# Split products for every weight chunk of layers 3 and 4: fills between attention steps go from fp32 to three fp32r products

## The chip, the cores and the metric

One core of one Trainium2 chip runs one launch of the whole program. The metric is the device time of that launch in microseconds (us), a median over runs. The engines are named as in the profile: PE is TensorE, DVE is VectorE, ACT is ScalarE, POOL is GpSimd, and SP issues most of the DMAs.

## What is computed

Four layers act on 256 tokens of width 2048, all in float32: a recurrent mixer, a mixture of experts, and then the two layers that the change touches. Cut to these two:

```
def even_layer(x, mem, ...):                     # layer 3
    h = rms_norm_2(x, norm_g) @ w_in
    gq, gk, gv, gb, ga, gg, dq, dk, dv, dg, mq, mg = split_cols(h, EV_SPLITS)
    y = jnp.concatenate([
        gdn_branch(gq, gk, gv, gb, ga, gg, ...),
        diff_attention(dq, dk, dv, dg, ...),     # 8 heads, two softmaxes each, mixed
        memory_attention(mq, mg, mem, ...),      # 4 heads
    ], axis=-1)
    return x + y @ w_out

def odd_layer(x, mem, positions, ...):           # layer 4
    h = rms_norm_2(x, norm_g) @ w_in
    sq, sk, sv, sg, mlq, ckv, kr, mlg, mq, mg = split_cols(h, OD_SPLITS)
    y = jnp.concatenate([
        window_attention(sq, sk, sv, sg, ...),   # 8 heads
        mla_attention(mlq, ckv, kr, mlg, ...),   # 8 heads, width 192
        memory_attention(mq, mg, mem, ...),      # 4 heads
    ], axis=-1)
    return x + y @ w_out
```

## The kernel before, in words

Each engine runs a program of its own, in the order in which it was written; semaphores (the kernel calls them events) tie them together, and the engines meet at the end of every `nc.Block`. All big weights are one stream of units. A unit is 1 MB: four chunks of 128 rows by 512 columns. SP loads units in order into a ring of eight slots (`stream`), and waits with a load until the slot's last unit is used.

A weight chunk is multiplied in one of two ways.

- **In a stage of its own** (`gemm_tokens`). ACT rounds the chunk to fp32r (the high part), DVE subtracts that from the chunk (the low part), and PE adds three fp32r products (high by high, low by high, high by low) for each of two token tiles. That is one step: six matmuls of 512 columns. The features are split in the same way at the start of each such stage. Four chunks of split weights are kept (`SPLIT_DEEP`), and sums of one 512-column block leave PSUM while the next block is multiplied.
- **As a fill** (`Fill`). A list of blocks of 512 columns is worked off in small portions that other stages call: `fill.multiply(pe, steps)` puts the next steps into PE's program, `fill.store_act` and `fill.store_dve` put the stores of finished blocks into the others'. A fill step multiplies the chunk straight from the ring in fp32, two matmuls of 512 columns, and asks nothing of ACT and DVE. There is one pair of PSUM banks for it, so PE waits at the start of a block until the last block has been stored.

`head_norm` normalizes heads (DVE squares, sums, scales), `times_silu` applies a gate and turns the result into features (`Turned`), and `attention` handles two heads at a time. One turn of it reads, per engine:

- PE: scores of two heads; fill portion 0; transposes of the next two heads' queries and keys (`begin`); portion 1; transposes of the probabilities; portion 2; sums with the values; portion 3. `steps=(a, b, c, d)` gives the sizes of the portions.
- DVE: scale, bias and maximum of two heads; store 0; stage the next two heads' queries and keys; store 1; for differential attention, mix the two softmaxes; store 2; write the outputs; store 3.
- ACT: exponentials; store 0; copy the transposed queries and keys; store 1; copy the transposed probabilities; stores 2 and 3.

The order of layer 3 is: the GDN branch, `gemm_tokens` over six blocks for the differential branch (96 steps), `head_norm`, `attention` (four turns), `head_norm` with gate, then memory attention (`head_norm`, two turns, `times_silu`) and a last `gemm_tokens` of 16 steps. In layer 4: `gemm_tokens` of 80 steps, window attention (`head_norm`, two calls of two turns, `times_silu`), `gemm_tokens` of 64 steps, a small product for the rotary key (`SmallProduct`, L2329), `gemm_tokens` of 16 steps, `head_norm`, `mla_rope`, `attention` (four turns), `times_silu`, `gemm_tokens` of 32 steps for the memory keys, memory attention, and `gemm_tokens` of 48 steps.

## Time and profile before

| what | value |
|---|---|
| time, median of 3 runs | 2788.83 us (2786.02 to 2790.07) |
| profiled execution, first to last instruction | 2787.4 us |
| PE busy with matmuls | 2598.2 us (93% of the span) |
| DVE busy | 1354.9 us (49%) |
| ACT busy | 976.6 us (35%) |
| HBM traffic | 189 GB/s over the span |

The profile gives no separate time for the profiled execution beyond its span; the median of the runs is 1.4 us above that span. Busy time counts the time that at least one instruction of an engine is in flight, and the ends of matmuls are modelled, so where PE's pace matters, the distance between starts is read and not the length of one. The first stage that the change touches begins at 1703 us of the span. An fp32 matmul of 512 columns stands in the trace as two records, an fp32r matmul as one. Idle time in the trace names who ended it; an engine name with a q is that engine's sequencer (a semaphore without an instruction, or the meeting at the end of a block).

### The profile page before, as it was taken

How to read it: one execution, taken by the hardware profiler on the slowest of the kernel's cores; microseconds unless marked ns; L12 is line 12 of the kernel's file. 1: busy time of each engine (PE TensorE's matmuls, PEld its weight loads, DVE VectorE, ACT ScalarE, POOL GpSimd, SP SyncE). 2: the span in 40 equal slices, each digit the busy share in tenths (PEclk: the TensorE clock that was granted, in tenths of full speed). 3: DMA queues.
4: the chain of work that ended last, by engine and by line, in shares of the span. 5: the costliest groups of instructions: out<-in, count | busy, mean ns of one | idle time of the engine just before them, and what ended most of it. 6: DMA issues, size and time to landing. Idle time of an engine off the chain costs nothing. (4 is left out here: it accounts for less than half of the span.)

```text
span 2787.4 us, 38289 instructions
## 1 busy us (share of the span) xinstructions
PE 2598.2 (93%) x14362; PEld 1770.8 (64%) x14362; DVE 1354.9 (49%) x2599; ACT 976.6 (35%) x1730; POOL 105.2 (4%) x117
## 2 busy tenths in 40 slices
PE   8999999999888889999998999989899989988999
PEld 7984555887544444448975766855467746845757
DVE  5654784665311112226764545554535445464535
ACT  5544122444122122225524424432235414423424
POOL 0001111020011100010000000000000000001000
PEclk9999999999999999999999999999999989999999
DMA  7754433554499999984431114543334523431432
GB/s 302 216 211 156 138 138 141 186 199 147 160 422 422 422 421 422 399 344 161 169 122 67 38 57 166 189 173 106 106 136 141 200 85 141 154 122 75 148 109 91
DMA packets 80312, 529.66 MB, mean 190 GB/s; under 512 B 9089, under 2 KB 13569, under 8 KB 18849
## 3 DMA queue, kind: packets, MB, share of 16 engines
q1 hardware_dynamic: 76128, 514.50, 48.9%
q0 software_dynamic: 3456, 11.02, 1.6%
q8 instruction: 99, 1.62, 0.2%
q10 hardware_dynamic: 576, 2.10, 0.2%
q14 instruction: 53, 0.43, 0.1%
HBM read 520.24 MB, written 7.34 MB: 189 GB/s over the span
## 5 line engine op out<-in xcount | busy, mean ns | idle before, releaser
L379 DVE TENSOR_TENSOR split_wl<-ring,split_wh 128x512 fp32r<-128x512 f32 x480 | 331.0, 698 | 227.5 <-ACT split_wh L353 225.7
L353 ACT ACTIVATE split_wh<-ring 128x512 fp32r<-128x512 f32 x480 | 301.0, 631 | 291.6 <-PE ps L329 291.6
L327 PE MATMUL ps<-split_wh,split_xh 128*128 128x512 f32 x960 | 375.5, 391 | 0.0
L329 PE MATMUL ps<-split_wh,split_xl 128*128 128x512 f32 x960 | 373.6, 389 | 0.0
L328 PE MATMUL ps<-split_wl,split_xh 128*128 128x512 f32 x960 | 373.5, 389 | 0.0
L2132 PE MATMUL ps<-ring,yT 128*64 128x256 f32 x2048 | 247.8, 387 | 52.4 <-DMA ring<-in_weights 48.3
L631 PE MATMUL ps<-ring,xT 128*128 128x512 f32 x512 | 241.8, 625 | 29.9 <-issue 7.2
L434 PE MATMUL ps<-features_xh,features_wh 128*128 128x256 f32 x832 | 236.7, 285 | 1.5 <-DVE features_wl L425 1.5
L2132 PEld LDWEIGHTS ps<-ring,yT 128*64 128x64 f32 x2048 | 137.7, 137 | 155.4 <-DMA ring<-in_weights 91.0
L436 PE MATMUL ps<-features_xh,features_wl 128*128 128x256 f32 x832 | 235.3, 283 | 0.0
L631 PE MATMUL ps<-ring,yT 128*128 128x512 f32 x448 | 206.3, 612 | 20.9 <-issue 11.1
L999 PE MATMUL ps<-ring,xT 128*128 128x512 f32 x512 | 222.0, 592 | 2.8 <-PEq L451 1.7
L329 PEld LDWEIGHTS ps<-split_wh,split_xl 128*128 128x128 f32 x960 | 180.2, 188 | 37.5
L327 PEld LDWEIGHTS ps<-split_wh,split_xh 128*128 128x128 f32 x960 | 180.2, 188 | 37.4
L328 PEld LDWEIGHTS ps<-split_wl,split_xh 128*128 128x128 f32 x960 | 180.2, 188 | 37.3
L631 PEld LDWEIGHTS ps<-ring,xT 128*128 128x128 f32 x512 | 99.5, 200 | 150.7 <-issue 142.2
L425 DVE TENSOR_TENSOR features_wl<-ring,features_wh 128x512 fp32r<-128x512 f32 x208 | 139.4, 691 | 83.3 <-ACT features_wh L419 79.5
L419 ACT ACTIVATE features_wh<-ring 128x512 fp32r<-128x512 f32 x208 | 130.2, 630 | 133.5 <-PE ps L436 133.5
L999 PEld LDWEIGHTS ps<-ring,xT 128*128 128x128 f32 x512 | 97.1, 190 | 120.6 <-issue 118.1
L631 PEld LDWEIGHTS ps<-ring,yT 128*128 128x128 f32 x448 | 84.6, 195 | 123.4 <-issue 123.3
L434 PEld LDWEIGHTS ps<-features_xh,features_wh 128*128 128x128 f32 x832 | 159.6, 192 | 2.9 <-DVE features_wl L425 2.6
L436 PEld LDWEIGHTS ps<-features_xh,features_wl 128*128 128x128 f32 x832 | 159.6, 192 | 0.0
(630 smaller groups left out, 3389.9 us busy)
## 6 DMA issues: line engine op xcount, KB each, us to landing
ring<-in_weights SPq DMA_DIRECT2D x468, 1024.0 KB, 5.1
x_res<-in_x SPq DMA_DIRECT2D x1, 2048.0 KB, 7.5
yT<-in_mem SPq DMA_DIRECT2D x1, 2048.0 KB, 15.7
rel_skew<-lru_feat POOLq DMA_DIRECT2D x1, 2048.0 KB, 50.7
mem_features<-yT ACTq DMA_DIRECT2D x4, 512.0 KB, 6.6
s_wb<-in_s_bc POOLq DMA_DIRECT2D x4, 512.0 KB, 4.0
s_wc<-in_s_bc POOLq DMA_DIRECT2D x4, 512.0 KB, 3.9
gate_bias<-in_gate_bias POOLq DMA_DIRECT2D x8, 256.0 KB, 3.9
```

What stands on the lines that cost most here:

```text
L327: nc.tensor.matmul(out, xh[:, kc, at], wh[:, c % deep, :], start=kc == 0, stop=False)
L328: nc.tensor.matmul(out, xh[:, kc, at], wl[:, c % deep, :], start=False, stop=False)
L329: last = nc.tensor.matmul(out, xl[:, kc, at], wh[:, c % deep, :], start=False, stop=kc == chunks - 1)
L353: nc.scalar.activation(wh[:, c % deep, :], raw(unit, turn, c), ACT.Copy).then_inc(w_high.sem, 1)
L379: last = nc.vector.tensor_tensor(wl[:, c % deep, :], raw(unit, turn, c), wh[:, c % deep, :], ALU.subtract)
L419: self.k.nc.scalar.activation(self.wh[:, c % self.deep, :], self.k.ring[:, slot, c * BLK:(c + 1) * BLK], ACT.Copy)\
L425: self.k.nc.vector.tensor_tensor(self.wl[:, c % self.deep, :], self.k.ring[:, slot, c * BLK:(c + 1) * BLK], self.wh[:, c % self.deep, :], ...
L434: nc.tensor.matmul(out, self.wh[:, c, cols], self.xh[:, kc, :], start=kc == 0, stop=False)
L436: last = nc.tensor.matmul(out, self.wl[:, c, cols], self.xh[:, kc, :], start=False, stop=kc == KC - 1)
L631: last = nc.tensor.matmul(k.ps[:, 6 + t, :], x[:, kc, t * P:(t + 1) * P], k.ring[:, slot, c * BLK:(c + 1) * BLK], start=kc == 0, stop=kc = ...
L999: mm = nc.tensor.matmul(k.ps[:, 6 + t, :], k.xT[:, kc, t * P:(t + 1) * P], k.ring[:, slot, c * BLK:(c + 1) * BLK], start=kc == 0, stop=kc ...
L2132: last = nc.tensor.matmul(k.ps[s * WIN:(s + 1) * WIN, p, 0:FF], window[:, p, kc, :], k.ring[:, slot, at:at + FF], start=kc == 0, stop=kc = ...
```

## The change

The features of a layer are split into high and low parts once (`k.layer`) and stay split. Every `gemm_tokens` that reads them takes them as they are (`whole=`). All fills except those of the GDN branch become `SplitFill`: a fill step is now three fp32r products per token tile, as in `gemm_tokens`, with the high part of each weight chunk made by ACT and the low part by DVE. These are put into the two engines' programs at the places where they stored blocks before. The buffer of split chunks is four deep, and at each such place the engines work up to four steps (`LEAD`) beyond what PE's portion has reached. Some blocks move from `gemm_tokens` stages into fills: two of the six blocks of the differential branch (its gate), two of the four blocks of MLA's input, and the product of MLA's output with `w_out`. The rotary key's small product moves to the end of the first `gemm_tokens` of layer 4. From layer 3 on the ring has four slots; the split features lie where the other four were.

Fill steps, before and now:

| place | before | now |
|---|---|---|
| layer 3, `head_norm` of differential attention | 8 | 8 |
| its four turns, portions (4,3,3,2), now (5,4,4,3) | 48 | 64 |
| its second `head_norm` | 8 | 8 |
| memory attention: norm, two turns, silu | 6 + 20 + 6 | 8 + 32 + 8 |
| layer 4, window: norm and bias, four turns, silu | 10 + 20 + 2 | 16 + 44 + 4 |
| MLA: norm and rope, four turns, silu | 20 + 8 + 4 | 22 + 36 + 6 |
| memory attention: norm, two turns, silu | 6 + 20 + 6 | 6 + 20 + 6 |
| all fills | 192 | 288 |
| all `gemm_tokens` steps from 1703 us on | 352 | 256 |

The core of the diff:

```
-def gemm_tokens(k, x, blocks, upb, finish_act, finish_dve, dve_after_act=False, ahead=None, deep=SPLIT_DEEP, beside=None, after=None):
+def gemm_tokens(k, x, blocks, upb, finish_act, finish_dve, dve_after_act=False, ahead=None, deep=SPLIT_DEEP, beside=None, after=None,
+                into=None, whole=None, parts=None, product=None):
...
+        if whole is not None:
+            xh, xl = whole
...
+class SplitFill:
+    LEAD = SPLIT_DEEP
...
+    def multiply(self, pe, steps):
...
+            if kc == 0:
+                pe.wait_ge(fill_a.sem, fill_a.at(n - 1))
+                pe.wait_ge(fill_v.sem, fill_v.at(n - 1))
...
+            pe.wait_ge(w_low.sem, w_low.at(step))
+            for t in range(NT):
+                out, at = k.ps[:, 6 + t, :], slice(t * P, (t + 1) * P)
+                mm(out, xh[:, kc, at], wh[:, c, :], start=kc == 0, stop=False)
+                mid = mm(out, xh[:, kc, at], wl[:, c, :], start=False, stop=False)
+                last = mm(out, xl[:, kc, at], wh[:, c, :], start=False, stop=kc == chunks - 1)
...
+            last.then_inc(w_used.sem, 1)
...
+    def make_highs(self, act, upto):
...
+        for step in range(self.high_at, min(upto, self.total)):
+            while self.act_done < len(self.blocks) and self.first[self.act_done + 1] <= step - self.LEAD:
+                self.take_act(act)
+            act.wait_ge(w_used.sem, w_used.at(step - SPLIT_DEEP))
...
+            k.nc.scalar.activation(k.parts[0][:, c, :], k.ring[:, slot, c * BLK:(c + 1) * BLK], ACT.Copy).then_inc(w_high.sem, 1)
...
+    def make_lows(self, dve, upto):
...
+            dve.wait_ge(w_high.sem, w_high.at(step))
+            k.nc.vector.tensor_tensor(k.parts[1][:, c, :], k.ring[:, slot, c * BLK:(c + 1) * BLK], k.parts[0][:, c, :], ALU.subtract)\
+                .then_inc(w_low.sem, 1)
...
+    def store_dve(self, dve, steps):
+        self.dve_at += steps
+        self.make_lows(dve, self.dve_at + self.LEAD)
...
-    gemm_tokens(k, k.xT, 6, KC // UNIT_KC, *store_tokens(k, pd))
+    gemm_tokens(k, None, 4, KC // UNIT_KC, *store_tokens(k, pd), whole=k.layer, parts=k.parts)
...
-              fill=fill, steps=(4, 3, 3, 2), turned=free.rearrange("p (j a) -> p j a", j=2))
+              fill=fill, steps=(5, 4, 4, 3), turned=free.rearrange("p (j a) -> p j a", j=2))
...
-        gemm_tokens(k, k.xT, 4, KC // UNIT_KC, *store_tokens(k, pq), ahead=lambda sp: load(k, sp, kr_w, k.dram["mla_kr_w"]))
+        gemm_tokens(k, None, 2, KC // UNIT_KC, *store_tokens(k, pq, 2 * BLK), whole=k.layer, parts=k.parts)
...
-    gemm_tokens(k, k.yT[:, 8:20, :], D // BLK, 3, *add_to_x(k, k.xT), dve_after_act=True,
+    gemm_tokens(k, None, D // BLK, 1, *add_to_x(k, out_spare), dve_after_act=True, whole=k.layer, parts=k.parts,
```

The first place shown is one turn of differential attention. First DVE's queue, from the second head's scores to the mix; `pe_b` is the event of the scores, `act_b` that of the exponentials. Before:

```order
L2740 SCALAR_TENSOR_TENSOR att_scores<-ps,diff_bias 128x512 [waits pe_b]
L2740 SCALAR_TENSOR_TENSOR att_scores<-ps,diff_bias 128x512
L2749 TENSOR_REDUCE att_stat<-att_scores 128x4
L2754 TENSOR_SCALAR att_stat<-att_stat 128x4
L2803 TENSOR_TENSOR att_q<-diff_q,rows_sb 128x256
L2803 TENSOR_TENSOR att_k<-diff_in,rows_sb 128x256
L2803 TENSOR_TENSOR att_q<-diff_q,rows_sb 128x256
L2803 TENSOR_TENSOR att_k<-diff_in,rows_sb 128x256
L2769 RECIPROCAL att_stat<-att_stat 128x4 [waits act_b]
```

The same place of DVE's queue now (`parts_wl` are low parts of weight chunks, `w_high` is the event of their high parts):

```order
L2937 SCALAR_TENSOR_TENSOR att_scores<-ps,diff_bias 128x512 [waits pe_b]
L2937 SCALAR_TENSOR_TENSOR att_scores<-ps,diff_bias 128x512
L2946 TENSOR_REDUCE att_stat<-att_scores 128x4
L2951 TENSOR_SCALAR att_stat<-att_stat 128x4
L804 TENSOR_TENSOR parts_wl<-ring,parts_wh 128x512 [waits w_high] x5
L3000 TENSOR_TENSOR att_q<-diff_q,rows_sb 128x256
L3000 TENSOR_TENSOR att_k<-diff_in,rows_sb 128x256
L3000 TENSOR_TENSOR att_q<-diff_q,rows_sb 128x256
L3000 TENSOR_TENSOR att_k<-diff_in,rows_sb 128x256
L804 TENSOR_TENSOR parts_wl<-ring,parts_wh 128x512 [waits w_high] x3
L3155 COPY diff_in<-ps 128x512 [waits fill_a,w_used]
L804 TENSOR_TENSOR parts_wl<-ring,parts_wh 128x512 [waits w_high]
```

The staging of the next heads now stands behind five low parts, and the mix (the next row, L2966) behind four more and the store of a block.

Next ACT's queue in a turn of the same attention, before (`dve_b` is DVE's event that the scores are scaled, `pe_a` and `pe_c` are PE's transposes):

```order
L2702 ACTIVATE att_scores,att_stat<-att_scores,att_stat 128x256 [waits dve_b]
L2702 ACTIVATE att_scores,att_stat<-att_scores,att_stat 128x256 x3
L2702 ACTIVATE att_scores,att_stat<-att_scores,att_stat 128x256 [waits dve_b]
L2702 ACTIVATE att_scores,att_stat<-att_scores,att_stat 128x256 x3
L2692 ACTIVATE yT<-ps 128x512 [waits pe_a] x2
L2712 ACTIVATE yT<-ps 128x512 [waits pe_c] x2
```

And now (`parts_wh` are high parts; `w_used` is PE's event that a step is done):

```order
L2899 ACTIVATE att_scores,att_stat<-att_scores,att_stat 128x256 [waits dve_b]
L2899 ACTIVATE att_scores,att_stat<-att_scores,att_stat 128x256 x3
L783 ACTIVATE parts_wh<-ring 128x512 [waits unit_loaded3,w_used] x4
L783 ACTIVATE parts_wh<-ring 128x512 [waits unit_loaded0,w_used]
L2889 ACTIVATE yT<-ps 128x512 [waits pe_a] x2
L783 ACTIVATE parts_wh<-ring 128x512 [waits unit_loaded0,w_used] x3
L3152 ACTIVATE diff_in<-ps 128x512 [waits w_used]
L783 ACTIVATE parts_wh<-ring 128x512 [waits unit_loaded1,w_used]
L2909 ACTIVATE yT<-ps 128x512 [waits pe_c] x2
```

High parts now stand between the exponentials and every later operation of the turn, each with a wait for a step of PE four steps earlier.

## Rows read from the trace of the kernel before

**Rows 1.** Windows: two `gemm_tokens` stages; busy us (count) of PE, PEld, DVE, ACT, POOL.

```profile
1703.50:1834.20 130.70, 130.70 (x578) 108.27 (x577) 72.33 (x104) 64.24 (x103) 0.00 (x0) 1.00 0.54 193
2716.50:2782.00 65.50, 65.50 (x290) 54.24 (x289) 38.39 (x56) 32.20 (x52) 0.00 (x0) 1.00 0.24 89
```

**Rows 2.** Page, costliest groups: low and high parts of weight chunks.

```profile
L379 DVE TENSOR_TENSOR split_wl<-ring,split_wh 128x512 fp32r<-128x512 f32 x480 | 331.0, 698 | 227.5 <-ACT split_wh L353 225.7
L353 ACT ACTIVATE split_wh<-ring 128x512 fp32r<-128x512 f32 x480 | 301.0, 631 | 291.6 <-PE ps L329 291.6
```

**Rows 3.** Timeline, end of a `gemm_tokens` step: start, length, engine, operation.

```profile
1820.41 0.39 PE L329 MATMUL ps<-split_wh,split_xl 128*128 128x512 f32 x1
1820.64 0.39 PE L327 MATMUL ps<-split_wh,split_xh 128*128 128x512 f32 x1
1820.84 0.63 ACT L353 ACTIVATE split_wh<-ring 128x512 fp32r<-128x512 f32 x1 [0.67 <-PE ps L329]
1821.50 0.69 DVE L379 TENSOR_TENSOR split_wl<-ring,split_wh 128x512 fp32r<-128x512 f32 x1 [0.61 <-ACT split_wh L353]
```

**Rows 4.** Windows, the stages with fills, layer 3, then layer 4.

```profile
1839.20:1857.30 18.10, 15.69 (x33) 6.61 (x33) 15.80 (x16) 1.38 (x2) 0.00 (x0) 0.90 0.65 225
1857.30:1972.60 115.30, 107.43 (x384) 56.52 (x384) 49.63 (x110) 30.00 (x86) 0.00 (x0) 0.99 0.31 109
1972.60:2004.60 32.00, 30.08 (x82) 14.71 (x82) 24.40 (x34) 8.08 (x10) 0.00 (x0) 0.95 0.35 126
2004.60:2070.20 65.60, 61.30 (x202) 32.67 (x202) 18.45 (x42) 15.63 (x33) 0.00 (x0) 0.97 0.29 102
2226.40:2249.00 22.60, 20.59 (x40) 8.50 (x40) 13.76 (x10) 0.22 (x1) 0.00 (x0) 0.87 0.51 177
2249.00:2334.50 85.50, 71.64 (x274) 42.71 (x274) 35.06 (x102) 25.56 (x64) 0.00 (x0) 0.92 0.21 74
2462.00:2508.20 46.20, 36.83 (x80) 15.63 (x80) 28.99 (x51) 3.93 (x7) 0.00 (x0) 0.93 0.26 91
2508.20:2589.50 81.30, 68.38 (x298) 40.47 (x299) 36.14 (x93) 28.02 (x63) 9.59 (x16) 0.96 0.19 71
2637.00:2648.10 11.10, 10.54 (x24) 4.48 (x24) 8.47 (x15) 1.50 (x2) 0.00 (x0) 1.00 0.26 79
2648.10:2714.50 66.40, 61.41 (x203) 33.08 (x203) 19.09 (x43) 15.68 (x34) 0.00 (x0) 0.97 0.30 103
```

**Rows 5.** Timeline, one turn of differential attention (from scores to scores).

```profile
1887.81 2.00 PE L2650 MATMUL ps<-yT 64*128 64x256 f32 x16
1888.99 1.29 DVE L2740 SCALAR_TENSOR_TENSOR att_scores<-ps,diff_bias 128x512 f32<-128x512 f32 x2 [4.09 <-PE ps L2650]
1889.73 7.13 PE L631 MATMUL ps<-ring,xT 128*128 128x512 f32 x16
...
1894.83 0.51 ACT L2702 ACTIVATE att_scores<-att_scores,att_stat 128x256 f32<-128x256 f32 x1 [0.87 <-DVEq L2758]
1894.88 0.42 DVE L2803 TENSOR_TENSOR att_q<-diff_q,rows_sb 128x256 f32<-128x256 f32 x1
1896.64 0.18 DVE L2769 RECIPROCAL att_stat<-att_stat 128x4 f32<-128x4 f32 x1
1896.70 0.38 PE L2637 MATMUL ps<-ident_sb,att_q 128*128 128x128 f32 x2
...
1898.74 0.18 DVE L2769 RECIPROCAL att_stat<-att_stat 128x4 f32<-128x4 f32 x1
...
1914.07 2.00 PE L2650 MATMUL ps<-yT 64*128 64x256 f32 x16
```

**Rows 6.** Timeline, memory attention: PE's wait for a block's store, and the matmuls behind it.

```profile
2652.13 3.60 PE L631 MATMUL ps<-ring,yT 128*128 128x512 f32 x8
...
2658.33 2.98 PE L631 MATMUL ps<-ring,yT 128*128 128x512 f32 x4 [2.61 <-issue]
```

**Rows 7.** Windows of 4 us around that wait.

```profile
2654.00:2658.00 4.00, 1.73 (x5) 0.42 (x3) 1.91 (x4) 2.01 (x7) 0.00 (x0) 1.00 0.27 61
2658.00:2662.00 4.00, 3.67 (x9) 1.95 (x10) 2.00 (x7) 0.00 (x0) 0.00 (x0) 0.64 0.48 201
```

More of the change, by code:

```diff
@@ L200, in load @@
         else:
[L201 removed]
+            src = k.dram["weights"][ds(turn * slots + unit, 1)].rearrange("u p n -> p (u n)")
         sp.dma_start(k.ring[:, slot], src).then_inc(k.unit_loaded[slot], 16)
[L204 to L211 removed]
+    while first < upto:
+        slots, _ = ring_of(first)
+        end = min(upto, LATE) if first < LATE else upto
+        turns = (end - first) // slots if first < LATE or first >= LATE + LATE_RING else 0
+        if turns >= 2:
+            with sp.Fori(0, turns) as i:
+                for s in range(slots):
+                    load(first + s, i)
+            first += turns * slots
+        else:
+            load(first)
+            first += 1
@@ L1689, in moe_places, with times_mem_gain @@
     return features[:, :, :], keys[:, :, :]
-def times_mem_gain(k, pool, features, gain):
+def times_mem_gain(k, pool, features, gain, chunks=range(KC)):
     pool.wait_ge(k.loaded, k.loads)
-    for c in range(KC):
+    for c in chunks:
         part = slice(c, c + 1)
@@ L2470, in _ @@
                 dve.drain()
+                if fill:
+                    fill.lows(dve, steps)
                 at = 0
@@ L2493, in _ @@
             def _(act):
+                if fill:
+                    fill.highs(act, min(steps, 6 + 2 * len(parts)))
                 act.wait_ge(ms.sem, ms.at(0))
@@ L2621, in _ @@
             def _(pool):
-                if beside is not None:
-                    beside(pool)
+                for i in range(turns):
+                    if beside is not None:
+                        beside(pool, i)
             @block.tensor
@@ L2922, in memory_keys, with memory_attention @@
     kv = k.sb(scope, f"{tag}_kv", [P, NT, 2 * MEM_HEADS * P])
-    gemm_tokens(k, features, 2, KC // UNIT_KC, *store_tokens(k, kv))
+    gemm_tokens(k, features, 2, KC // UNIT_KC, *store_tokens(k, kv), parts=k.parts)
     return kv
-def memory_attention(k, tag, qg, kv, gain_q, gain_k, fill):
+MEM_STEPS = {"evm": (8, (5, 5, 4, 2), 8), "odm": (6, (3, 3, 2, 2), 6)}
+def memory_attention(k, tag, qg, kv, gain_q, gain_k, fill, out):
     n = MEM_HEADS * P
+    first, steps, last = MEM_STEPS[tag]
     with ExitStack() as inner:
```

312 lines of the change are left out of this document (222 added, 90 removed).

## Prediction, made before the run

> **What bounds the kernel now.** I read the profile's page first (PE busy 93% of the span), then PE's timeline from 1703 us on to find the stages, then one row of windows per stage, and last one attention turn on all three engines. The reader is to see four things.
>
> PE never stops in a `gemm_tokens` stage: 130.7 us for 96 steps and 65.5 us for 48 [rows 1]. So a split step costs PE 1.36 us there, while ACT and DVE, at 0.63 and 0.70 us for it [rows 2], have slack.
>
> An fp32 fill step is four records, 0.43 us apart (16 records, 7.13 us with the modelled tail [rows 5]): 1.72 us of PE and nothing of ACT or DVE.
>
> In an attention turn PE is nearly always at work, because DVE's and ACT's chains run under its portions. The turn shown lasts 26.3 us (1887.81 to 1914.07): 12 steps of 1.72 and 5.4 of attention matmuls make 26.0. DVE's statistics for two heads take 5.9 us (1888.99 to 1894.88), under portion 0; staging ends at 1896.64, before PE asks at 1896.70; the mix follows at once, 2.1 us a head, under portion 1 [rows 5].
>
> In the stages of `head_norm` DVE is as long as PE: 15.8 busy of 18.1 us in the first [rows 4].
>
> **The change on PE alone.** All 544 steps stay. 192 fill steps fall from 1.72 to 1.36: -69 us. 96 steps change place at the same price. If PE stayed the bound, that would be all: 2720.
>
> **What it does to the order.** A step's split chunk goes into the place of the step four before it. At each store place ACT and DVE make parts up to four steps beyond PE's portion, and the last of these needs PE's last step of that portion. Both engines are in order, so whatever stands behind a store place starts only when PE has finished the portion. The refill chain is in [rows 3]: PE's step ends at 1820.64, ACT starts at 1820.84, DVE at 1821.50 and is done at 1822.19: 1.55 us. Thus what ran under PE's portions now runs after them, and PE, whose four ready chunks are spent, waits for it.
>
> The Trainium skill ("TensorE: Matmul & The Clock Gate", the table at its top) says that ScalarE's and VectorE's queues are strictly first in, first out. Going by that rule no later staging or mix can pass a waiting low part, which speaks against this change; if they could pass, the time would be the 2720 above. The turn's rows agree as far as they go: every operation starts in program order [rows 5].
>
> **One turn of differential attention, portions 5, 4, 4, 3.** T is the start of the scores.
> - DVE is free of its last low part at T+1.6, has both heads' statistics at +7.5 (5.9), ACT the exponentials at +9.5 (four, 2.1). Only then comes the fifth chunk's high part: ready with its low part at +10.9. PE, after 1.9 of scores and four steps, stood there at +7.3: wait 3.6. Portion 0 ends at 12.3.
> - Refill 1.55, staging 0.9 a head (1.76 for two [rows 5]): transposes from 14.8 to 16.1, 2.9 of it waiting.
> - Portion 1, 5.4, with one block end in it. High part, copy, low part, copy: 2.3 us (ACT 0.6 and 0.6, DVE 0.7 and 0.7, 0.2 before). To 23.8.
> - Refill 1.55, mix 2.1 a head, the second transposes behind it: to 30.0, 5.3 waiting.
> - Portion 2, values, portion 3: 5.4 + 1.8 + 4.1, to 41.3.
>
> Three turns of 41.3, the last without staging 37.6, 2 for splitting the GDN features between them, 5 for head and tail: 168.5 where 115.3 stood [rows 4]: **+53**.
>
> **The other attentions.** Their softmax is divided after the sums, so PE waits for no mix. Left are the staging wait (3; 4.4 in window attention, where four high parts stand behind the exponentials) and the block ends: 2.9 where a block is added to x; before it cost 2.6 [rows 6]. A turn is 5.4 of attention (9.9 in MLA) plus steps times 1.36 plus these.
> - Layer 3 memory: turns 33.4 and 31.7, silu 14.5, ends 4.4: 84.0 against 65.6: **+18.4**, for 14 more steps.
> - Window: 2 x (25.3 + 21.6), one inner block end 2.3, silu 11.2, ends 6.5: 113.8 against 85.5: **+28.3**, 26 more.
> - MLA: 3 x 25.5 + 20.1, block ends 6.1, ends and POOL's gain beside it 9.6, silu 14.9: 127.2 and 0.5 for the meeting, against 81.3: **+46.4**, 30 more.
> - Layer 4 memory, no more steps: 24.8 + 21.6 + 19.6 = 66.0 against 66.4: **-0.4** [rows 4].
>
> **The norms.** DVE's low parts, 0.62 us each back to back (0.70 with the latency [rows 2]), add to a DVE that already sets the end. First norm: 12 of them (8 and 4 ahead) 7.5, first chunk's chain 1.3, last refill partly: **+9.5**. The two norms of the row at 1972.6: 2 x 8 low parts 9.9, less 0.7 in which DVE waited: **+9.2**. Window norm and bias: 20 low parts 12.4, less 6 of idle on DVE (13.8 of 22.6 busy), and a copy: **+6.7**. MLA norm and rope: 12 low parts in the norm, +8.2; in rope PE's steps stand behind 6.7 us of DVE sums but the store that came after rope comes earlier, +2.7: **+10.9**. Layer 4 memory: 10 low parts and the first chain: **+7.0** [rows 4].
>
> **Moved out of the bound stages.** 96 `gemm_tokens` steps, as many as the first row: **-130.7** [rows 1]. The features' splits at stage starts hide behind warm-up matmuls: 0. The rotary product no longer overlaps a norm's sums but stands behind a stage, about +6 there and -3 where it was: **+3.2**.
>
> **Sum:** 53 + 18.4 + 28.3 + 46.4 - 0.4 + 9.5 + 9.2 + 6.7 + 10.9 + 7.0 + 3.2 - 130.7 = **+61.5 us**.
>
> **The clock.** Behind a PE wait of 2.61 us four records take 2.98 us; eight took 3.60 before it. The granted clock of that stretch is 0.64, part of it at 1.2 instead of 2.4 GHz, after 1.00 [rows 6, 7]. At half pace a stretch of some 4 us does 2 us of work, so it costs about 2. New waits as long as that: some 12 in differential attention, some 10 elsewhere. Bounds: none of them lowers the clock further (0), or each costs 2 (+44). Rows 4 have granted clocks of 0.87 to 1.00 with such waits in them already, and cold stretches inside a later wait cost nothing, so I take +12.
>
> The Trainium skill (same title, "What's actually happening") says that the throttled state is the default and that only activity releases it. If that rule bites at every such wait, the time is 2787.4 + 61.5 + 44 + 1.4 = 2894; the one wait shown agrees [rows 7].
>
> **Result:** 2787.4 + 61.5 + 12 = 2861 for the profiled span; the runs' median is 1.4 above the span: **2862 us**.
>
> **Rivals.**
> - *PE stays the bound* (faster, 2720 to 2785). It needs that parts are ready ahead of PE's portions. The stalls in my sum are 61.5 + 69 = 130 us; the change breaks even when they are under 69, about half. For it speaks that low parts cost half a step on DVE and attention's DVE work leaves 65 us of 115 free [rows 4]; against it, that the free time lies under PE's portions, where the order now lets nothing but refills run. Chance 0.11, and 0.03 for within 0.2%.
> - *The waits are real but lighter* (2795 to 2835): block ends and refills overlap more, the clock costs nothing. +61.5 less a third of the norms' and block ends' 50 is +45; with fewer staging waits +20. Chance 0.16.
> - *The clock pays for every wait* (2885 to 2920): +61.5 and up to 44, or more where slow portions delay refills. 0.10.
> - *A ring of four starves* (over 2890): a unit of 1 MB is used up in four steps, 5.4 us, and 193 GB/s were moved at that pace with eight slots [rows 1]. One us of wait per unit over the 72 units of the fills: +72 more. For it: half the lead. Against: four units are still 22 us of PE. 0.03.
> - *The order does not change* is excluded: the queues show it.
>
> My forecast, 2835 to 2885, has the rest, 0.57. The range 2812 to 2898 takes in the zero clock term and most of its upper bound and leaves out the faster side and the far end. A difference under 0.2% (5.6 us) is what a measurement of this kernel can't tell from none. Faster 0.11, same 0.03, slower 0.86.
>
> **What would show it.** PE idle before the fifth matmul step of portion 0, before the staged transposes and before the transposed probabilities in differential attention, ended by DVE, 12 us and more a turn; turns of 40 us or more. Other attentions with one staging wait a turn. Norm stages ended by DVE. Three `gemm_tokens` stages shorter by 43.6 us each at unchanged pace. More windows of low granted clock. Wrong would be: portions that run on while DVE stages, or low parts that come well before PE needs them.

## The result, and the profile after

| kernel | time, median | ratio to before, 95% interval | profiled span | mean granted clock |
|---|---|---|---|---|
| before | 2789.1 us (2786.0 to 2790.1) | | 2787.4 us | 0.985 |
| after | 2907.8 us (2905.3 to 2909.4) | 1.0428 [1.0414, 1.0443] | 2903.6 us | 0.961 |

The change makes the kernel 119 us slower. The forecast was 2862 us, 73 us slower, with a range up to 2898: the direction was right, the time lies 10 us beyond the range.

The page of the changed kernel: span, busy times, the clock in 40 slices of the span, and the three groups of the fills' split steps.

```profile
span 2903.6 us, 39591 instructions
...
PE 2589.0 (89%) x14740; PEld 1879.6 (65%) x14740; DVE 1471.9 (51%) x2795; ACT 1087.1 (37%) x1922; POOL 107.4 (4%) x117
...
PEclk9999999999999999999999999788999999988989
...
L759 PE MATMUL ps<-parts_wh,layer_xh 128*128 128x512 f32 x576 | 253.9, 441 | 96.6 <-DVE parts_wl L804 43.0
L804 DVE TENSOR_TENSOR parts_wl<-ring,parts_wh 128x512 fp32r<-128x512 f32 x288 | 192.8, 694 | 249.1 <-ACT parts_wh L783 247.7
...
L783 ACT ACTIVATE parts_wh<-ring 128x512 fp32r<-128x512 f32 x288 | 175.1, 628 | 270.3 <-PE ps L761 253.5
```

No engine is the bound: PE waits for a low part (L804), DVE for a high part (L783), ACT for PE's step (L761). A part costs ACT and DVE the same 0.63 and 0.69 us as in [rows 2]; what changed is who waits for whom. The clock row has a 7 and two 8s where layer 3's differential attention stands.

The stages with fills, as windows: the same stages in the same order as [rows 4] (columns as there), without the `gemm_tokens` stretches between them. Here a stage reaches to the first matmul of the next, so some lengths hold up to 6 us more than the same stage in [rows 4]; the attention named below has the same edges in both.

```profile
1786.80:1817.80 31.00, 14.20 (x55) 11.03 (x53) 24.82 (x33) 10.43 (x17) 0.00 (x0) 0.83 0.51 174
1817.80:2007.20 189.40, 138.74 (x576) 106.91 (x576) 92.62 (x176) 71.01 (x153) 0.00 (x0) 0.83 0.24 87
2007.20:2052.10 44.90, 30.00 (x123) 24.10 (x123) 36.77 (x54) 19.11 (x29) 0.00 (x0) 0.86 0.28 103
2052.10:2144.90 92.80, 80.37 (x349) 64.84 (x349) 45.29 (x83) 40.31 (x75) 0.00 (x0) 0.90 0.31 114
2297.00:2342.00 45.00, 32.69 (x161) 26.95 (x159) 28.64 (x35) 13.52 (x23) 0.00 (x0) 0.89 0.42 143
2342.00:2466.60 124.60, 104.98 (x485) 84.89 (x485) 64.34 (x148) 54.07 (x113) 0.00 (x0) 0.92 0.28 104
2545.20:2605.90 60.70, 38.79 (x139) 28.84 (x137) 48.30 (x85) 21.31 (x36) 0.00 (x0) 0.86 0.26 91
2605.90:2742.90 137.00, 113.30 (x513) 86.88 (x513) 67.95 (x140) 56.84 (x113) 11.68 (x16) 0.91 0.27 99
2787.80:2806.90 19.10, 9.95 (x44) 7.65 (x42) 15.92 (x27) 7.64 (x13) 0.00 (x0) 0.92 0.16 62
2806.90:2876.30 69.40, 58.31 (x264) 46.84 (x265) 34.36 (x67) 30.96 (x60) 0.00 (x0) 0.90 0.30 106
```

Differential attention takes 189.4 us instead of 115.3 [rows 4], and PE is busy 138.7 of them. Its work there is 64 steps of 1.36 and four times 5.4, that is 108.6. So 50.7 us are idle, and 30 us are PE at work but slow. The granted clock of the row is 0.83; it was 0.99.

One turn of it, on three engines (start, length, engine, operation, idle time before it and who ended it):

```profile
1867.44 2.00 PE L2847 MATMUL ps<-yT 64*128 64x256 f32 x16
...
1874.76 0.39 PE L761 MATMUL ps<-parts_wh,layer_xl 128*128 128x512 f32 x1
1878.30 0.50 PE L759 MATMUL ps<-parts_wh,layer_xh 128*128 128x512 f32 x1 [3.15 <-DVE parts_wl L804]
...
1879.17 0.63 PE L759 MATMUL ps<-parts_wh,layer_xh 128*128 128x512 f32 x1
1879.60 0.63 PE L760 MATMUL ps<-parts_wl,layer_xh 128*128 128x512 f32 x1
1880.03 0.63 PE L761 MATMUL ps<-parts_wh,layer_xl 128*128 128x512 f32 x1
...
1880.70 0.63 ACT L783 ACTIVATE parts_wh<-ring 128x512 fp32r<-128x512 f32 x1 [1.62 <-PE ps L761]
1881.36 0.69 DVE L804 TENSOR_TENSOR parts_wl<-ring,parts_wh 128x512 fp32r<-128x512 f32 x1 [1.31 <-ACT parts_wh L783]
1881.97 0.42 DVE L3000 TENSOR_TENSOR att_q<-diff_q,rows_sb 128x256 f32<-128x256 f32 x1
1882.80 0.69 PE L2834 MATMUL ps<-ident_sb,att_q 128*128 128x128 f32 x2 [2.14 <-DVEq L2928]
...
1891.55 0.47 PE L759 MATMUL ps<-parts_wh,layer_xh 128*128 128x512 f32 x1 [2.09 <-ACT diff_in L3152]
...
1896.88 1.12 PE L2865 MATMUL ps<-ident_sb,att_scores 128*128 128x128 f32 x4 [3.36 <-DVEq L2977]
...
1898.95 1.11 PE L2865 MATMUL ps<-ident_sb,att_scores 128*128 128x128 f32 x4 [0.96 <-DVEq L2977]
...
1912.71 2.00 PE L2847 MATMUL ps<-yT 64*128 64x256 f32 x16
```

The reader is to see the chain that the prediction drew: PE's last step of the portion, then ACT's high part, DVE's low part, only then DVE's staging (L3000), and PE's transposes (L2834) behind it. The four waits stand where they were forecast, and are 3.15, 2.14, 2.09 and 3.36 + 0.96 = 11.7 us in this turn, where the prediction had 3.6, 2.9, 2.3 and 5.3 = 14.1. But the turn takes 45.3 us and not 41.3 (its neighbours 47.7 and 46.9), because behind the waits records stand 0.43 us apart and not 0.23 (1879.17, 1879.60, 1880.03): 1.2 GHz and not 2.4.

The same over everything from the first changed stage to the last, before and after:

```profile
1703.50:2782.00 1078.50, 1005.87 (x3964) 688.23 (x3963) 546.65 (x955) 395.68 (x730) 9.59 (x16) 0.97 0.38 134
```

```profile
1699.50:2898.30 1198.80, 997.95 (x4343) 796.96 (x4342) 663.82 (x1151) 505.53 (x922) 11.68 (x16) 0.91 0.35 124
```

Idle time rose from 72.6 to 200.8 us: +128.2 (the prediction's stalls were 130). PE's work should have fallen by 69 and fell by 7.9: +61 of slow matmuls. -69 + 128 + 61 = +120; the first changed stage began 4 us earlier, which makes the +116 of the two spans. So at a first look the clock, for which the prediction had put 12 us and at most 44, is half of the loss. A busy time does not say, though, whether a slow matmul delays anything: that is for the experiments.

### The profile page after: what moved, and what is told of

The parts are those of the page before. It is cut to its first block and busy times, and to the rows that moved or that the text cites. A ratio compares the mean times of both kernels' runs of the same rounds, so it can differ in the third digit from the quotient of the medians.

```text
span 2903.6 us, 39591 instructions
## 1 busy us (share of the span) xinstructions
PE 2589.0 (89%) x14740; PEld 1879.6 (65%) x14740; DVE 1471.9 (51%) x2795; ACT 1087.1 (37%) x1922; POOL 107.4 (4%) x117
## 5 line engine op out<-in xcount | busy, mean ns | idle before, releaser
L759 PE MATMUL ps<-parts_wh,layer_xh 128*128 128x512 f32 x576 | 253.9, 441 | 96.6 <-DVE parts_wl L804 43.0
L804 DVE TENSOR_TENSOR parts_wl<-ring,parts_wh 128x512 fp32r<-128x512 f32 x288 | 192.8, 694 | 249.1 <-ACT parts_wh L783 247.7
L783 ACT ACTIVATE parts_wh<-ring 128x512 fp32r<-128x512 f32 x288 | 175.1, 628 | 270.3 <-PE ps L761 253.5
L760 PE MATMUL ps<-parts_wl,layer_xh 128*128 128x512 f32 x576 | 243.0, 422 | 0.0
L761 PE MATMUL ps<-parts_wh,layer_xl 128*128 128x512 f32 x576 | 241.4, 419 | 0.0
L1178 PE MATMUL ps<-ring,xT 128*128 128x512 f32 x512 | 222.0, 592 | 2.8 <-PEq L488 1.7
L759 PEld LDWEIGHTS ps<-parts_wh,layer_xh 128*128 128x128 f32 x576 | 119.3, 207 | 139.0 <-DVE parts_wl L804 50.7
L413 DVE TENSOR_TENSOR split_wl<-ring,split_wh 128x512 fp32r<-128x512 f32 x208 | 145.1, 707 | 97.6 <-ACT split_wh L387 96.6
L387 ACT ACTIVATE split_wh<-ring 128x512 fp32r<-128x512 f32 x208 | 130.9, 633 | 131.7 <-PE ps L360 131.7
L413 DVE TENSOR_TENSOR parts_wl<-ring,parts_wh 128x512 fp32r<-128x512 f32 x176 | 120.0, 691 | 94.4 <-ACT parts_wh L387 94.1
L387 ACT ACTIVATE parts_wh<-ring 128x512 fp32r<-128x512 f32 x176 | 109.7, 632 | 113.5 <-PE ps L360 106.8
L761 PEld LDWEIGHTS ps<-parts_wh,layer_xl 128*128 128x128 f32 x576 | 119.2, 207 | 27.8
L472 PE MATMUL ps<-features_xl,features_wh 128*128 128x256 f32 x448 | 126.7, 283 | 0.0
```

The costliest lines, as they stand in the source:

```text
L387: nc.scalar.activation(wh[:, c % deep, :], raw(unit, turn, c), ACT.Copy).then_inc(w_high.sem, 1)
L413: last = nc.vector.tensor_tensor(wl[:, c % deep, :], raw(unit, turn, c), wh[:, c % deep, :], ALU.subtract)
L759: mm(out, xh[:, kc, at], wh[:, c, :], start=kc == 0, stop=False)
L760: mid = mm(out, xh[:, kc, at], wl[:, c, :], start=False, stop=False)
L761: last = mm(out, xl[:, kc, at], wh[:, c, :], start=False, stop=kc == chunks - 1)
L783: k.nc.scalar.activation(k.parts[0][:, c, :], k.ring[:, slot, c * BLK:(c + 1) * BLK], ACT.Copy).then_inc(w_high.sem, 1)
```

## The experiments

All times are medians; where not said otherwise the computation is unchanged. In the edits, comments behind a `#` are this document's. "Loss" is what the change adds to the kernel before.

**Filler matmuls in the waits.** Two runs, differing in the number of fillers:

```diff
+                    if fill and n == 0 and comps == 2:
+                        fill.multiply(pe, SPLIT_DEEP)
+                        keep_busy(k, pe, 0, 12)        # second run: 8
+                        fill.multiply(pe, steps[0] - SPLIT_DEEP)
...
+                        keep_busy(k, pe, 0, 8)         # second run: 5
                         begin(i + 1)
...
+                    def at_block_end():
+                        if more:
+                            pe.wait_ge(qk_copied.sem, qk_copied.at(0, i + 1, 2))
+                        keep_busy(k, pe, 0, 8)         # second run: 4
...
+                            pe.wait_ge(shifted.sem, shifted.at(j, i, 2))
+                            keep_busy(k, pe, 2 + 2 * j, (13, 4)[j])   # second run: (7, 3)
                             pe.wait_ge(mixed.sem, mixed.at(j, i, 2))
```

> The changed kernel with nothing taken away: PE gets more instructions. In the attentions it runs filler matmuls (128x256, 0.23 us each warm) in places where it waits: 12 ahead of the fifth step of a differential turn, 8 ahead of the staged transposes, 8 at a block end in portion 1, 13 and 4 ahead of the two heads' transposed probabilities. Theory (half of the loss is idle time, half is the clock that falls behind each wait): the waits stay, but the matmul records behind them are 0.23 us and not 0.43; the differential attention falls from 189 to about 165 us, the kernel by about 35 us (20 to 50), to about 2873. Rival (the slow steps lie under DVE's chains and cost nothing, all of the loss is waits): within 6 us of the changed kernel, 2908. A filler that outlasts its wait would make it slower.

2897.2 us, 1.0381 [1.0363, 1.0398]: 11 us less than the changed kernel, nearer to the rival's number, and it proves nothing either way, since I had put a filler at 0.23 us where it takes 0.43 (it is two records). In the turn from 1871.49 us PE was never idle and the records of the steps stood 0.23 us apart, but the fillers took 20 us a turn for 12 us of waits. The turn stayed at 47.0.

> The first filler run again with shorter fillers: there each filler matmul took 0.43 us and not the 0.23 that I had put, so the fillers (5.3, 3.6, 3.6, 5.8 and 1.9 us in a turn) outlasted the waits of 3.1, 2.1, 2.1, 3.4 and 1.4 us while every record of PE ran at 0.23. Now 8, 5, 4, 7 and 3 of them: 3.5, 2.2, 1.7, 3.0 and 1.3 us. Theory (about half of the loss is the clock behind the waits): a differential turn falls from 46.9 to about 42 us, the differential attention by 18 to 24 us, the kernel by about 30, to 2878 (2862 to 2890). Rival (cold steps lie under the other engines' chains): 2897 or more, as in the first filler run.

2868.3 us, 1.0284 [1.0267, 1.0301]: 39.5 us less than the changed kernel, with more work for PE. Of the timeline of one turn:

```profile
1862.67 2.00 PE L2853 MATMUL ps<-yT 64*128 64x256 f32 x16
...
1870.22 3.61 PE L293 MATMUL ps<-rows_sb,ident_sb 128*128 128x256 f32 x16
...
1875.05 2.32 PE L293 MATMUL ps<-rows_sb,ident_sb 128*128 128x256 f32 x10
...
1886.56 3.18 PE L293 MATMUL ps<-rows_sb,ident_sb 128*128 128x256 f32 x14
...
1904.10 1.14 PE L2853 MATMUL ps<-yT 64*128 64x256 f32 x8
```

From scores to scores it is 41.4 us: with the clock kept up (L293 are the fillers; the granted clock of this attention is 0.99), the turn is the 41.3 that the prediction summed for the order alone. Part of that match is luck. The five gaps that the fillers stand in measure 3.3, 2.3, 2.3, 3.5 and 1.6 us, 13.0 in sum, where the prediction had 14.1 of waits, and the work between them is 28.5 us, where it had 27.2. The gaps are also 1 us longer than the 12.0 us that PE waits in an average turn of the changed kernel: a slow PE comes later to its waits and waits less there, so part of what the slow records cost is given back. The clock in the attentions costs 39.5 us of the 119 by the medians, and 33.6 by the spans of the two profiled runs. Where a filler outlasts its wait, the clock's cost is more than that.

**Parts two steps ahead, not four.** At the first two store places of a differential turn, the first of the others:

```diff
-        self.make_lows(dve, self.dve_at + self.LEAD)
+        self.make_lows(dve, self.dve_at + lead)        # 2 at these places, 4 at the others; ACT the same
```

> The changed kernel, where in an attention turn ACT and DVE split only two steps beyond PE's portion at its first store place (in differential attention at its first two) and not four; the rest of the parts follow behind the staging and the mix. Theory (the last refills, which need PE's last steps, hold up staging and mix): the wait before the staged transposes falls by about 1 us a turn, that before the transposed probabilities by about 2.5, a differential turn by about 4.5 us; 13 to 15 us there, about 1.2 us a turn over 11 turns elsewhere, with a few us of clock: about 25 us (15 to 40) less, 2883. Rival (DVE's own work is the chain and refills wait for nothing): no change, 2908.

2847.7 us, 1.0214 [1.0194, 1.0234]: 60 us less, more than twice what I expected. One turn:

```profile
1867.94 0.79 PE L759 MATMUL ps<-parts_wh,layer_xh 128*128 128x512 f32 x1 [3.14 <-DVE parts_wl L804]
...
1870.67 0.52 PE L2835 MATMUL ps<-ident_sb,att_q 128*128 128x128 f32 x2
...
1879.37 0.66 PE L2866 MATMUL ps<-ident_sb,att_scores 128*128 128x128 f32 x4 [0.23 <-DVEq L2978]
```

The wait ahead of the staged transposes is gone and the one ahead of the transposed probabilities fell from 3.36 to 0.23 us; the turn is 36.3 to 38.7 us. All waits of a turn together fell from 12.0 to 6.2 us on average, and that took almost 9 us off it (37.8 on average, after 46.6). The other 3 us fit the slow stretches that stood behind those waits; no run separates the two.

**The ring of four alone.**

```diff
+LATE_RING = 4
+LATE = sum(b * u for _, b, u in STREAM[:[name for name, _, _ in STREAM].index("ev_mem_v")])
...
+    return (RING, 0) if unit < LATE else (LATE_RING, LATE)
```

> The kernel before, with the weight ring of layers 3 and 4 cut from eight slots to four as in the change, and nothing else. Theory (four units are still over 20 us of PE): no change, 2789 within 4 us. Rival (a ring of four starves PE): PE waits for the ring's loads in the gemm stages and the fills, 20 us or more slower.

2787.1 us, 0.999 [0.9981, 1.0]: no cost in the kernel before, whose late units (from `ev_mem_v` on) now use four slots. In the changed kernel's own trace no wait of PE, ACT or DVE from 1699.5 us on is put down to a load. That rival of the prediction is excluded.

**The moved blocks as fp32 products.** The changed kernel's order; this run leaves the features' low parts out of the fills' products:

```diff
-                mm(out, xh[:, kc, at], wh[:, c, :], start=kc == 0, stop=False)
-                mid = mm(out, xh[:, kc, at], wl[:, c, :], start=False, stop=False)
-                last = mm(out, xl[:, kc, at], wh[:, c, :], start=False, stop=kc == chunks - 1)
+                last = mm(k.ps[:, 6 + t, :], xh[:, kc, t * P:(t + 1) * P].bitcast(F32), k.ring[:, slot, c * BLK:(c + 1) * BLK],
+                          start=kc == 0, stop=kc == chunks - 1)
```

> The changed kernel's order and its moved blocks, but each fill step is one fp32 product of the features' high parts with the ring's weights, as before the change; the weights are not split in the fills, so ACT and DVE make no parts there, and the features' low parts are left out of these products. Theory (the loss comes from the refills in order and the clock behind their waits, not from the move): 96 moved steps at 0.36 us more are +35 on the kernel before, less up to 25 us of PE's idle time in window and latent attention that they fill: about 2810 (2798 to 2826). Rival (the move itself, its block ends and the loads, makes the waits): over 2850.

2819.3 us, 1.0109 [1.0092, 1.0126]. The move alone costs 30 us, almost all of 96 steps at 0.36 us more; the idle time of layer 4 that it might have filled was hardly filled. The split products, which save PE 104 us against this kernel (288 steps at 0.36 less), cost 88 us on top.

**No parts in the fills.** ACT and DVE split only the first four chunks of each fill, and PE multiplies these again and again, so what the fills compute is not the product of the weights; the run serves for its time alone.

```diff
-            act.wait_ge(w_used.sem, w_used.at(step - SPLIT_DEEP))
...
-            k.nc.scalar.activation(k.parts[0][:, c, :], k.ring[:, slot, c * BLK:(c + 1) * BLK], ACT.Copy).then_inc(w_high.sem, 1)
+            if step < SPLIT_DEEP:
...
+                k.nc.scalar.activation(k.parts[0][:, c, :], k.ring[:, slot, c * BLK:(c + 1) * BLK], ACT.Copy).then_inc(w_high.sem, 1)
```

> The changed kernel with the fills' part work left out: ACT and DVE split only the first four weight chunks of each fill, and PE multiplies these over and over, with its full number of fp32r products and its waits for the loads; what it computes in the fills is thus not the product of the weights. Theory (the whole loss is the parts' order and work; PE's own work is 69 us less than before): 2720 to 2745, the time that the first rival of the prediction gives. Rival (something else in the change costs time, such as the moved blocks' ends, the ring or fp32r products beside the attentions): 2780 or more.

2753.2 us, 0.9874 [0.9858, 0.9889]: the making and placing of parts costs 155 us, all of the loss and more. It also corrects the first rival: with parts for nothing the change would gain 36 us, not 69. From the first changed stage to the last:

```profile
1700.30:2745.90 1045.60, 950.32 (x4344) 769.54 (x4343) 487.91 (x879) 343.94 (x651) 10.32 (x16) 0.97 0.40 142
```

PE idles 95.3 us where it idled 72.6, and is busy 950.3 where it was busy 1005.9, 55.6 less and not 69. A likely reason for the idle time, not tested, is that a shorter step covers less of the statistics, mixes and norms beside it.

**Another place for the parts.** A table for each attention says how PE's steps are dealt to the four portions, and up to which step of the turn DVE and ACT have made parts at each of 8 and 7 points (ahead of, between and behind the two heads' statistics, stagings, mixes, and so on). The table came from adding up the three queues with the durations of the rows. Work, depth of the parts and number of steps stay. A finished block is also stored one part earlier than in the changed kernel, in this run and in the next.

```diff
-              fill=fill, steps=(5, 4, 4, 3), turned=free.rearrange("p (j a) -> p j a", j=2))
+              fill=fill, steps=(5, 4, 4, 3), turned=free.rearrange("p (j a) -> p j a", j=2), plan=((7, 7, 2, 0), (0, 6, 7, 7, 12, 15, 19, 20), (6, 9, 10, 17, 11, 16, 9)))
...
                     for j in pair:
+                        dve_parts(dve, i, j)    # make_lows up to the table's step, ahead of head j's statistics
...
-            while self.dve_done < len(self.blocks) and self.first[self.dve_done + 1] <= step - self.LEAD:
+            while self.dve_done < len(self.blocks) and self.first[self.dve_done + 1] <= step - 3:
```

> The changed kernel with the same work, the same four-deep parts and the same PE steps per turn, but another order inside the attentions: PE's steps are dealt to the four portions anew (differential attention 7, 7, 2, 0 for 5, 4, 4, 3), and ACT and DVE make parts at more places of a turn (between the two heads' statistics, exponentials, stagings and mixes), nowhere parts whose slots come free only with PE's last steps ahead of work that PE waits for; a filled block is evicted one part earlier. Theory (the loss is the place of the refills in two strictly ordered queues, and the clock behind the waits, not the parts' work): by adding up the three queues with the rows' durations a differential turn falls from 41 us (47 with the clock) to about 30, the other attentions by 8, 17, 18 and 6 us, so with the clock about 110 us less than the changed kernel: 2800 (2775 to 2835), about the kernel before. Rival (ACT's and DVE's part work is what PE waits for, wherever it stands): no better than two steps of lead gave, 2848 or more.

2782.0 us, 0.9979 [0.9969, 0.9989]: 126 us less than the changed kernel, 0.2% less than before. The first of the plan's three lists deals PE's steps. Differential attention as a window, and PE's wait at a block end in a turn, the only one over 0.5 us left in it:

```profile
1819.40:1953.80 134.40, 122.29 (x586) 99.24 (x587) 94.02 (x178) 69.84 (x154) 0.00 (x0) 0.93 0.35 126
```

```profile
1870.57 0.47 PE L759 MATMUL ps<-parts_wh,layer_xh 128*128 128x512 f32 x1 [1.84 <-ACT diff_in L3175]
```

134 us instead of 189, with DVE and ACT as busy as in the changed kernel (94.0 and 69.8 against 92.6 and 71.0). So in this attention the engines' work was never the bound, the order was.

> The fifth run's kernel, but PE's portions are those of the change (5, 4, 4, 3 in differential attention); only the places at which ACT and DVE make their parts differ from the changed kernel. Theory (it is the refills' place, not the split of PE's steps): the queues' sums give 13 us more than the fifth run in differential attention and about 8 in the others: 2803 (2790 to 2820), so 105 of the 126 us come from the places alone. Rival (the dealing of PE's steps did it): within 15 us of what two steps of lead gave, 2833 or more.

2804.0 us, 1.0064 [1.0048, 1.0079], 1 us from the expectation. With PE's portions left at 5, 4, 4, 3 and as they were in the other attentions, the places of the parts, with the earlier store of a block, give 104 of the 126 us. What the earlier store alone gives was not measured.

**Fillers in the norms.**

```diff
                     fill.multiply(pe, steps)
+                    keep_busy(k, pe, 5, hold)          # 16, 10 or 14; 12 or 4 ahead of the transposes in a gating
...
+                    if i == 0:
+                        keep_busy(k, pe, 0, 5)         # at the start of each attention
```

> The reordered kernel of the fifth run with filler matmuls (0.43 us each) where PE still waits long in and between the norms: 16 at the end of the first norm of layer 3, 12 ahead of the transposes of the second, 10 at the end of each memory norm, 14 at the end of the latent norm, 4 ahead of the transposes in two gatings, 5 at the start of each attention. Theory (each of some 10 long waits is followed by a stretch at half pace): 1 to 2 us each, together 8 to 20 us less than 2782: about 2768 (2760 to 2776), below the kernel before by 0.7%. Rival (the cold steps behind these waits lie under DVE's chains of the first turn, or the fillers outlast their waits): 2780 or more.

2781.4 us, 0.9976 [0.9967, 0.9985]: nothing, the rival's case. The two profiled runs, without and with these fillers:

```profile
core 0: 2784.3 us, clock 0.976
```

```profile
core 0: 2783.4 us, clock 0.985
```

The mean clock is back where it was before the change, and the time has not moved. The rival named two reasons, and the two traces show some of each. The first norm, up to the first scores, is 35.8 us and not 33.6; 1.5 of that is the five fillers at the start of the attention, which outlast their wait. The first differential turn behind it, now free of its slow start, is 32.3 us and not 33.4, so little of that start had cost time. Up to the next `gemm_tokens` stage layer 3 is 3.4 us shorter, and the segment of MLA is 2.6 us longer. How the rest divides was not taken apart. A mean clock is no measure of what the clock costs.

**Low parts by POOL in the norms.** In the norms, the bias stage and the rotary stage POOL makes the low parts, 84 of the 288 by the trace (the expectation says some 50); DVE's own calls there then find none left to make.

```diff
+            @block.gpsimd
+            def _(pool):
+                if isinstance(fill, SplitFill):
+                    fill.pool_lows(pool, steps)        # the same subtraction by gpsimd.tensor_tensor
```

> The reordered kernel of the fifth run, where the low parts of the fills are made by POOL and not by DVE in the norms, the bias stage and the rotary stage (some 50 of 288); all other low parts stay on DVE. In these stages DVE sets the end: they are 8, 13, 9, 12 and 6 us longer than in the kernel before. POOL's nearest row is 1.06 and 0.61 us for a product of 128x256, so one low part may take 1.2 to 2.1 us, against 1.36 of PE. Theory (DVE's part work in the stages that it bounds is the rest of the loss): 25 to 35 us less than 2782: about 2752 (2742 to 2765). Rival (POOL and DVE slow one another when both read two tensors, or POOL's low parts become the chain that PE waits for): DVE's squares and sums take longer by as much as is taken off it, 2775 or more.

2791.1 us, 1.0005 [0.9996, 1.0014]: 9 us slower than the run without it (7 by the two ratios, since the two were measured beside separate runs of the kernel before). The groups of the first norm, POOL's and DVE's of this run, then DVE's of the run without:

```profile
L832 POOL TENSOR_TENSOR parts_wl<-ring,parts_wh 128x512 fp32r<-128x512 f32 x12 | 21.2, 1797 | 560.6 <-ACT parts_wh L783 560.6
...
L2687 DVE TENSOR_TENSOR diff_q<-diff_q,head_stat 128x1024 f32<-128x1024 f32 x2 | 4.5, 2292 | 0.1
...
L2670 DVE TENSOR_TENSOR yT<-diff_in 128x1024 f32<-128x1024 f32 x2 | 4.2, 2104 | 0.1
```

```profile
L2667 DVE TENSOR_TENSOR diff_q<-diff_q,head_stat 128x1024 f32<-128x1024 f32 x2 | 2.4, 1222 | 0.1
L2650 DVE TENSOR_TENSOR yT<-diff_in 128x1024 f32<-128x1024 f32 x2 | 2.4, 1222 | 0.1
```

DVE's products of two tensors take 2.1 to 2.3 us beside POOL's and 1.22 without. That is the first half of the rival, and in layer 3 it does not outweigh the gain: from the first norm to the next `gemm_tokens` stage the run is 3.3 us shorter. The loss is in layer 4, 3.8 us in the window segment and 2.4 in that of MLA. In the window segment the second half of the rival shows:

```profile
2253.10 9.85 POOL L832 TENSOR_TENSOR parts_wl<-ring,parts_wh 128x512 fp32r<-128x512 f32 x6
2254.31 2.58 DVE L2687 TENSOR_TENSOR swa_in<-swa_in,head_stat 128x1280 f32<-128x1280 f32 x1
2263.30 0.77 PE L759 MATMUL ps<-parts_wh,layer_xh 128*128 128x512 f32 x1 [3.55 <-PEq L2656]
```

DVE is done with the norm at 2256.9 and POOL only at 2263.0, and the block ends with POOL. PE, after a wait of 3.55 us there, runs the steps of the bias stage with records 0.43 us apart up to 2269. The segment of MLA was not taken apart.

**A looser handover at a block's end**, in the reordered kernel and in the kernel before. PE waits for DVE's store only ahead of the second token half, and DVE copies its bank beside ACT and not behind it where a block is stored by token:

```diff
                 pe.wait_ge(fill_a.sem, fill_a.at(n - 1))
-                pe.wait_ge(fill_v.sem, fill_v.at(n - 1))
...
             for t in range(NT):
+                if kc == 0 and t == 1:
+                    pe.wait_ge(fill_v.sem, fill_v.at(n - 1))
...
-        dve.wait_ge(fill_a.sem, fill_a.at(n))
+        if self.blocks[n][1] != KC:
+            dve.wait_ge(fill_a.sem, fill_a.at(n))
```

> The reordered kernel of the fifth run with a looser handover at the end of a filled block: PE starts the next block's three products of the first token half when ACT has taken that bank, and waits for DVE only ahead of the second half; where the block is stored by token and not added to x, DVE copies its bank beside ACT and not behind it. Theory (24 block ends cost PE 1.5 to 2.4 us each where another engine's queue is in the way): about 0.6 us each, less where nothing waited: 8 to 14 us less than 2782, about 2771. Rival (the parts behind the block end are late as well, so PE only waits one step further on): within 4 us of 2782.

2773.4 us, 0.9941 [0.9927, 0.9954]: 9 us less than without it, the fastest kernel here of those that compute the weights' product.

> The kernel before, nothing of the change in it, with the looser handover at a filled block's end that the tenth run has (PE waits for DVE only ahead of the second token half; DVE does not stand behind ACT where a block is stored by token). It tells how much of the tenth run's 0.6% belongs to the handover and how much to the change. Theory (before, a block end waits where an engine's queue is in the way, a few times 1.5 to 5 us): 3 to 10 us less than 2788, about 2783, so that the change in its reordered form is worth some 10 us beside it. Rival (the handover cost the old kernel as much as the new one): 2776 or less, and the change is worth nothing.

2775.4 us, 0.9956 [0.9942, 0.9969]: the rival's case. The kernel before gains 0.44% by the same edit, the reordered one stands at 0.59%; the intervals overlap. The handover is the gain, and the change in its best order is worth 0.1 to 0.2%, no more than can be told from nothing.

## Why the prediction was off, by its own steps

**What bounds the kernel, and what the change does on PE alone: right.** Each of the three `gemm_tokens` stages is 43.5 to 45.1 us shorter (forecast 43.6, and 3 for the rotary product at one of them).

**The order: right in mechanism, a little small.** The refills of four parts hold up staging and mix as the prediction said: with two steps of lead the wait ahead of the staged transposes is gone, and parts at other places take 104 us off the whole. The Trainium skill ("TensorE: Matmul & The Clock Gate", the table at its top) has ScalarE's and VectorE's queues strictly first in, first out; the turn's rows agree (L3000 starts at 1881.97, behind the low part that had waited until 1881.36), and so does the run with two steps of lead. Segment by segment (from the end of one `gemm_tokens` stage to the start of the next, us longer than before):

| segment | forecast, no clock | measured | measured with fillers |
|---|---|---|---|
| layer 3: norms, differential and memory attention | 90.1 | 120.1 | 96.2 |
| layer 4: rotary product, window norm, bias, attentions | 41.0 | 54.2 | 47.6 |
| layer 4: latent norm, rotary stage, attention | 57.3 | 66.4 | 63.7 |
| layer 4: memory attention | 6.6 | 7.3 | 6.3 |
| the three shorter stages | -133.7 | -132.1 | -132.1 |
| two other `gemm_tokens` stages | 0 | 4.4 | 3.7 |
| start of the first changed stage | 0 | -4.0 | -2.9 |
| sum (61.5 in the prediction, which rounded less) | 61.3 | 116.3 | 82.5 |

With fillers in the attentions' waits each segment is within 7 us of its forecast, and the sum is 21 us over. The order's terms were 18 to 21 us too small in all: 6 to 7 in each of the three large segments, and 4 of matmul pace that nobody had put down. The first norm, +8.0 for a forecast of 9.5, and the last segment fit; in the others I did not take the rest apart.

**The clock: the step that failed.** It read "so I take +12", between bounds of 0 and 44. The fillers measure 39.5 us in the attentions alone, 27.5 more than I took; with the 18 of the order that is the whole miss of 46 (by the profiled runs 22 and 21, of 43). The error was to scale from a case with one wait, 2.61 us in [rows 6]: I counted 22 new ones "as long as that" and then let most of them cost nothing, because the windows of [rows 4] held such waits at clocks of 0.87 to 1.00. But in the differential attention of the kernel before PE waited 1 us or longer three times; here it does so 19 times, four or five in each turn of 45 us, nearly all of 1.4 to 3.4 us, and the granted clock of the stage is 0.83. Over the four segments of the table with attentions the count rose from 25 to 58, so the 22 were too few as well. The Trainium skill (same title, "HAM oscillation — how this bites in real kernels") describes this: a kernel whose matmul groups are separated by waits starts every group slow and pays each time. Its example has waits of some 3 to 5 us; here the rows behind waits of 3.15, 2.14 and 3.36 us are 0.43 us apart, so they agree, and shorter waits did it too. The rival "the clock pays for every wait", 2885 to 2920 with a chance of 0.10, has the measured time in its range. Its clock term came near; without the 18 us by which the order was too small it would have come to some 2890.

**The other rivals.** "PE stays the bound" was false as the change stands; the placed parts show that it could have been half true: 2782. Its lower end, 2720, is out of reach even with no parts at all (2753). "A ring of four starves" is excluded. That stalls must stay under 69 us to break even was too generous for the same reason: with no parts at all the gain is 36 us.

## What to carry to other kernels

When work is put into in-order queues ahead of other work, look at the last piece of it: if that piece needs the consumer's last step, everything behind it starts when the consumer has finished, and the cover is gone. Making the same parts at other points of the same turn, with blocks stored one part earlier, was worth 104 us here, 126 with PE's steps dealt anew. Price a wait of TensorE at its length plus the slow stretch behind it when several such waits stand close together, and test it by fillers that fit the wait, since a mean clock tells nothing of its cost. And run a side edit on the old kernel too: three quarters of what the best version gains belongs to it.

## What the runs showed of the hardware

- DVE's operation on two tensors of 128x1024 in SBUF took 1.22 us alone and 2.1 to 2.3 us while POOL subtracted two tensors; POOL's own 128x512 took 1.80 us on average in the first norm, with a median of 1.30 over all 84. The Trainium skill ("GPSIMD Engine Reference", "Specifications") says that GpSimd shares its SBUF interfaces with VectorE and contends with instructions that have two SBUF inputs; these rows agree.
- In two `gemm_tokens` stages whose weights, features or parts lie elsewhere since the change, the same matmuls run 3% slower at a granted clock of 1.00, with no wait between them: 87 records in 20 us in the window stage where the kernel before had 90 in the second row.

```profile
2234.00:2254.00 20.00, 20.00 (x87) 16.11 (x86) 9.85 (x15) 9.57 (x16) 0.00 (x0) 1.00 0.52 193
```

```profile
2162.00:2182.00 20.00, 20.00 (x90) 16.55 (x89) 10.98 (x16) 9.59 (x17) 0.00 (x0) 1.00 0.54 176
```

It costs 4.4 us. The ring of four alone does not show it (109.02 us for the stage, as before). The runs with fp32 fills and with no parts in the fills do show it (0.232 and 0.233 us from one start to the next in the window stage, 0.227 before), so the parts made in the fills are not its cause. Five other `gemm_tokens` stages that the change touches keep 0.227 to 0.229. Where it comes from stays open.
